# Turning attention probabilities as quarter products in an RWKV/attention/MoE block

## The chip, the cores and the metric

The kernel runs on one core of one Trainium2 chip. Its time is the device time of one launch; for the kernel before it is 640.22 us, the median of three runs (640.09 to 640.49).

## The reference

One decoder layer on 256 tokens of width 1024, in float32. `h = rms_norm(x)` goes through one input projection whose columns feed three mixers: causal pooling, RWKV-7 time mixing (8 heads of 64) and sparse attention (16 query heads, 4 key/value heads; compressed blocks, selected blocks and a sliding window). The mixers are projected, gated and summed, then comes a mixture of 32 experts. What the change touches is in the middle of it:

```
ls = einsum('bghqd,bgqkd->bghqk', qb, k_sel) + bias_s          # scores
ps = masked_softmax(ls, mask_s)                                # probabilities
o_s = einsum('bghqk,bgqkd->bghqd', ps, v_sel)                  # weighed values
...
def step(state, inp):                                          # RWKV-7, one token
    r_t, w_t, k_t, v_t, kk_t, a_t = inp
    sa = einsum('bhvk,bhk->bhv', state, -kk_t)
    state = state * w_t + sa * (kk_t * a_t) + v_t * k_t
    return state, einsum('bhvk,bhk->bhv', state, r_t)
```

The probabilities come out of the softmax with queries on the partitions, and the product with the values contracts over keys, so they have to be transposed ("turned") first. The RWKV recurrence is computed in tiles of 128 tokens with products of 64x64, and also needs some of its operands turned.

## The kernel before

Five instruction streams (TensorE = PE, VectorE = DVE, ScalarE = ACT, GpSimd = POOL, SyncE = SP) are written out by hand in one fixed order each, and meet at semaphores. Matmul results go to eight PSUM banks of 128x512 float32. A table, `plan`, made by the calls `hand(name, bank)`, says which result takes which bank and as which user of it; `begin(name)` lets PE wait until all earlier users of the bank are released (`bank_free`), `end` marks it full (`bank_full`), and the reader (ACT through `give`, or DVE) releases it after its last read.

Attention works in 24 units, slots n = 0 to 23 (`UNITS`, six for each of four groups of heads, u = n mod 6). A slot n on PE holds, in this order:

1. `early(step)`: the first half of an RWKV step, in most slots products of 64x64 (`chunkwise` on line 846, `products` on 968, line 810, line 826);
2. `turn(g, u)`: the four 128x128 blocks of slot n's probabilities `prob` turned into bank 2 (line 955, inside `turned`);
3. half of this slot's share of the merge gate products (`gate_matmuls`, lines 620, 128x128 tiles with 256 columns, two records each in the trace);
4. `late(step)`: the second half of the RWKV step, again 64x64 or 128x128;
5. in odd slots `weigh` (line 1004, values times turned probabilities); in even slots `scores` (line 984) of slots n+2 and n+3 into banks 0 and 1, both of which have to be free before the first;
6. the other half of the gates and `after(step)`.

In every sixth slot (u = 0) a further RWKV step stands ahead of this. ACT in slot n does its part of the RWKV step, then `exps(n+1)` (line 1609), then copies the turned probabilities of n from the bank (line 1435, `tok<-bank`) and releases it. DVE in slot n does its RWKV part, then `gated(n+1)` (the product that makes `prob` of n+1 final, line 1810 `tok<-tok,small`), then `logits(n+2)` (line 2038), which reads the scores of n+2 and releases their bank.

The RWKV tiles are i = 0 and 1. The step "turn" has an early part, two groups of four transposes (`bf`, `kf`, into banks 5 and 6), which ACT copies to `btok` and `ktok`, and a late part, two more groups into banks 7 and 5. For tile 0 it stands ahead of all slots, at 140 us; for tile 1 it is the step of slot 6.

Of the kernel before, what the change touches and what calls it, by code (L numbers as in the profile page):

```python
# [22 lines left out]
F32 = mybir.dt.float32  # L23
# [4 lines left out]
P = 128  # L28
D = 1024
S = 256  # L30
NT = S // P
# [5 lines left out]
DH = 64  # L37
# [147 lines left out]
def build_layer(nc, x, params, consts, front, experts, g_final, out, bias_rows):  # L185
    ctx = ExitStack()
    with ctx:
# [151 lines left out]
        gdiag = gspread[:, 1, :]  # L339
        gchan = small[:, 224:232]  # L340

        bank = [ctx.enter_context(nc.psum_tensor(f"bank{b}", [P, 512], F32)) for b in range(8)]
        total = [[bank[2], bank[6]], [bank[3], bank[7]]]


# [37 lines left out]
        def hand(name, b):  # L383
            assert name not in plan
            plan[name] = (b, nth(b))
# [19 lines left out]
        hand("ks", 0)  # L405
        hand("kcb", 7), hand("vcb", 6)
        hand("bonus0", 4), hand("bonus1", 5)

        def hand_early(step):
            if step is None:  # L410
# [76 lines left out]
        for n, (g, u) in enumerate(UNITS):  # L487
            if u == 0:
                step = next(steps)
                if g == 0:  # L490
                    hand("cT", 2)
                hand_early(step)
                hand_late(step)
                hand(f"o{g}", 7 if g == NG - 1 else 3)
                hand_gates(next(slot))
                hand_after(step)
            step = next(steps)
            hand_early(step)
            hand(f"pT{g}{u}", 2)
            hand_late(step)  # L500
            if n % 2 == 0 and n + 2 < len(UNITS):
                hand("s%d%d" % UNITS[n + 2], 0), hand("s%d%d" % UNITS[n + 3], 1)
            hand_gates(next(slot))
            hand_after(step)
# [8 lines left out]
        hand("places", 5)  # L513

        before_loop = [nth(b) for b in range(8)]


        def full(eng, name):
# [72 lines left out]
        def _(pe):  # L591
# [193 lines left out]
            def early(step):  # L785
                if step is None:
                    return
                kind, i, which = step
                ts = slice(i * P, (i + 1) * P)
                if kind == "turn":  # L790

                    if i == 0:
                        pe.wait_ge(q["rwkv_ready"], 1)
                    for w_, src in enumerate((bf, kf)):
                        turned(f"tok{i}{w_}", [src[:, m, ts] for m in range(4)])
                elif kind == "products":
                    products(i, 0)
                elif kind == "level":
                    n = which
                    pe.wait_ge(q["x_ready"], 5 * i + n + 1)  # L800
                    pe.wait_ge(q["lmask_ready"], 6 * i + n + 2)
                    chunkwise((f"W{i}{n}", lmask[(n + 1) % 2], xinv, 0, 1))
                elif kind == "local":
                    pe.wait_ge(q["xu_ready"], 2 * (i + 1))
                    rbank = [begin(f"rx{i}{c}") for c in range(2)]
                    for h in range(RH):
                        m, p = h // 2, h % 2
                        for c in range(2):
                            rows = slice(64 * c, 64 * c + 64)
                            last = pe.matmul(rbank[c][64 * p:64 * p + 64, m * CH:(m + 1) * CH],  # L810
                                             rhs[rows, h, 0, :], amat[rows, h, 1, :], start=True, stop=True)
                            if h == RH - 1:
                                end(last, f"rx{i}{c}")
                elif kind == "scan":
                    n = 2 * i + which
                    pe.wait_ge(q["rx_ready"], 2 * (i + 1))
                    pe.wait_ge(q["fc_ready"], n + 1)
                    pe.wait_ge(q["zeroed"], 3)
                    if n:
                        pe.wait_ge(q["state_ready"], n)  # L820
                    if n < NCH - 1:
                        o = begin(f"st{i}{which}")
                        for h in range(RH):
                            m, p = h // 2, h % 2
                            rows = slice(64 * p, 64 * p + 64)
                            last = pe.matmul(o[rows, m * DH:(m + 1) * DH], fc[rows, which, m, 0, :],
                                             state[rows, n % 2, m, :], start=True, stop=True)
                        end(last, f"st{i}{which}")
                elif kind == "finish":
                    pe.wait_ge(q["lora_g_ready"], 1)  # L830
                    o = begin(f"gup{i}")
                    for m in range(4):
                        last = pe.matmul(o[:, m * P:(m + 1) * P], pr("g_up", 96)[:, m * P:(m + 1) * P], mix[0:96, 13, ts],
                                         start=True, stop=True)
                    end(last, f"gup{i}")
# [115 lines left out]
            def turned(name, parts):  # L951

                o = begin(name)
                for b, part in enumerate(parts):
                    last = pe.transpose(o[:, b * P:(b + 1) * P], part, ident)  # L955
                end(last, name)

            def products(i, pair):

                obank = [begin(f"A{i}{pair}{p}") for p in range(2)]  # L960
                for mm_ in range(2):
                    m = 2 * pair + mm_
                    for j, left in enumerate((bf, kf)):
                        for c in range(2):
                            ts = slice(i * P + 64 * c, i * P + 64 * c + 64)
                            for p in range(2):
                                rows = slice(64 * p, 64 * p + 64)
                                last = pe.matmul(obank[p][64 * c:64 * c + 64, mm_ * 256 + j * P:mm_ * 256 + (j + 1) * P],  # L968
                                                 left[rows, m, ts], ar[rows, m, i, :, 64 * c:64 * c + 64],
                                                 start=True, stop=True)  # L970
                                if mm_ == j == c == 1:
                                    end(last, f"A{i}{pair}{p}")
# [16 lines left out]
            def turn(g, u):  # L989

                n = g * 6 + u
                pe.wait_ge(q["prob_ready"], n + 1)

                turned(f"pT{g}{u}", [prob[:, n % 2, s * P:(s + 1) * P] for s in (0, 2, 1, 3)])

            def weigh(g, u, o):

# [435 lines left out]
        def _(act):  # L1433
# [5 lines left out]

            count = {}  # L1440

            def give(ins, name, job):

                count[name] = count.get(name, 0) + 1
                ins.then_inc(q[name], 1)
                act.wait_ge(q[name], count[name])
                act.sem_inc(bank_free[plan[job][0]], 1)  # L1447

            def to_hT(n):

# [107 lines left out]
            def early(step):  # L1558
                if step is None:
                    return  # L1560
                kind, i, which = step
                if kind == "turn":
                    for w_, dst in enumerate((btok, ktok)):
                        b0 = full(act, f"tok{i}{w_}")
                        give(copy(dst, b0[:, :]), "tok_ready", f"tok{i}{w_}")
                elif kind == "level":
                    name = f"W{i}{which}"
                    b0 = full(act, name)
                    give(copy(winv, b0[:, :].rearrange("p (h t) -> p h t", h=RH)), "w_ready", name)
                elif kind == "solve":  # L1570
                    b0 = full(act, f"w0{i}")
                    give(copy(rhs[:, :, 1, :], b0[:, :].rearrange("p (h v) -> p h v", h=RH)), "rhs_ready", f"w0{i}")
# [70 lines left out]
            for n, (g, u) in enumerate(UNITS):  # L1643
                if u == 0:
                    step = next(steps)
                    gate_tanh(gates_done(next(slot) - 1))
                    if g == 0:
                        turned_compressed()
                    early(step)
                    late(step)  # L1650
                step = next(steps)
                gate_tanh(gates_done(next(slot) - 1))
                early(step)
                if n + 1 < len(UNITS):
                    exps(*UNITS[n + 1])
                b0 = full(act, f"pT{g}{u}")
                give(copy(probT[:, n % 2, :], b0[:, :]), "probT_ready", f"pT{g}{u}")
                late(step)
            gate_tanh(gates_done(DURING - BEFORE - 1))

# [142 lines left out]
        def _(dve):  # L1803
# [221 lines left out]
            def logits(g, u):  # L2025
# [2 lines left out]
                p = u % 2  # L2028
                b0 = full(dve, f"s{g}{u}")
                if n >= 2:  # L2030
                    b, cnt_ = plan[f"pT{(n - 2) // 6}{(n - 2) % 6}"]
                    dve.wait_ge(bank_full[b], cnt_ + 1)
                nb, w = (4, P) if u < 2 else (2, S)
                for b in range(nb):
                    bs = slice(b * w, (b + 1) * w)
# [483 lines left out]
```

## Time and profile before

| | |
|---|---|
| median of 3 runs | 640.22 us |
| the profiled execution | 640.59 us, span of its instructions 638.8 us |
| PE busy | 596.5 us, 93% of the span |
| DVE busy | 216.1 us, 34% |
| ACT busy | 142.7 us, 22% |
| HBM read | 157.07 MB, 248 GB/s over the span |
| mean granted TensorE clock | 0.977 of full speed |

The span is divided into 40 slices on the profile's page; attention lies in slices 12 to 21; the experts' weights come in from slice 22 on, at up to 425 GB/s. Times of instructions are microseconds from the span's start. A matmul in float32 has two records in the trace, a transpose has one; matmuls overlap, so what a group costs is read from its start to the start of what follows, not from the sum of its durations. The tile in the array (as 64*64) stands ahead of the shape.

### The profile page before, as it was taken

The page shows a single profiled execution, that of the slowest core. Times are in us where ns is not written, and L with a number is a line of the kernel's source. Part 1 is how long each engine was busy: PE and PEld are TensorE (multiplying, and loading weights), DVE is VectorE, ACT ScalarE, POOL GpSimd, SP SyncE. Part 2 cuts the span into 40 slices and gives each one's busy share as a digit, 9 for nine tenths or more (in the row PEclk, how much of TensorE's full clock was granted, in tenths as well). Part 3 has the DMA queues.
Part 4 walks back from the last instruction along what each step waited for, and adds up shares of the span by engine and source line. Part 5 has one row for each costly group of instructions (what it writes and reads, how often), then busy time and mean ns, then how long its engine had stood idle before and what let it go on. Part 6 is the DMA issues. An engine that isn't in the chain of part 4 may idle for free.

```text
span 638.8 us, 11809 instructions
## 1 busy us (share of the span) xinstructions
PE 596.5 (93%) x4968; PEld 432.8 (68%) x4968; DVE 216.1 (34%) x586; ACT 142.7 (22%) x366; POOL 19.9 (3%) x23
## 2 busy tenths in 40 slices
PE   8999999999999999999999999998988988958694
PEld 7988887878877877778888888884434533414331
DVE  3152448625334766356220322233111111101022
ACT  3110234042234453444330000001110111000023
POOL 1000000000200103001000000000000000000000
PEclk9999999999999999999999999998999989969798
DMA  8584344841211121102336997978999999999993
GB/s 326 196 324 171 124 145 158 316 139 67 88 47 69 68 68 68 68 27 107 122 97 261 422 421 280 425 315 313 424 419 419 422 420 421 420 421 421 422 390 123
DMA packets 27416, 158.95 MB, mean 249 GB/s; under 512 B 3025, under 2 KB 7265, under 8 KB 9569
## 3 DMA queue, kind: packets, MB, share of 16 engines
q1 hardware_dynamic: 24352, 137.71, 55.1%
q10 hardware_dynamic: 3008, 20.45, 7.7%
q8 instruction: 41, 0.67, 0.4%
q14 instruction: 15, 0.11, 0.1%
HBM read 157.07 MB, written 1.07 MB: 248 GB/s over the span
## 4 chain that ended last, share of the span: by engine, by line
PE 61%; issue 22%; DMA 7%; SPq 4%; DVE 3%; ACT 2%; POOL 0%; POOLq 0%; DVEq 0%; ACTq 0%
PE bank L620 27%; PE bank L1235 7%; DMA ring<-experts 6%; PE bank L1299 4%; SPq L583 4%; PE bank L1244 4%; PE bank L1308 3%; PE bank L846 3%; PE bank L652 2%; PE bank L955 2%; PE bank L984 2%; PE bank L1004 1%; DVE work L1810 1%; PE bank L968 1%; DMA table<-params 1%
## 5 line engine op out<-in xcount | busy, mean ns | idle before, releaser
L620 PE MATMUL bank<-hT,ring 128*128 128x256 f32 x864 | 199.4, 383 | 0.4 <-ACTq L1447 0.3
L620 PEld LDWEIGHTS bank<-hT,ring 128*128 128x128 f32 x864 | 159.6, 190 | 30.4 <-issue 10.6
L620 PE MATMUL bank<-yT,ring 128*128 128x256 f32 x256 | 55.4, 379 | 0.0
L620 PEld LDWEIGHTS bank<-yT,ring 128*128 128x128 f32 x256 | 48.6, 190 | 6.6
L1810 DVE TENSOR_TENSOR work<-bank,table 128x512 f32<-128x512 f32 (+1 forms) x22 | 11.6, 544 | 97.2 <-PE bank L1244 90.5
L1299 PE MATMUL bank<-ring,work 128*32 128x512 f32 (+1 forms) x192 | 36.0, 667 | 7.8 <-DMA yT<-experts 6.6
L1244 PEld LDWEIGHTS bank<-work,tok 128*128 128x128 f32 x256 | 31.0, 196 | 10.2 <-issue 10.2
L1435 ACT ACTIVATE work<-bank 128x512 f32<-128x512 f32 (+2 forms) x45 | 23.4, 519 | 55.1 <-PE bank L1299 42.5
L1244 PE MATMUL bank<-work,tok 128*128 128x128 f32 x256 | 32.5, 282 | 0.5 <-DVEq L2319 0.5
L1308 PE MATMUL bank<-work 128*128 128x512 f32 (+1 forms) x68 | 30.4, 584 | 1.3 <-ACT work L1435 0.7
L1609 ACT ACTIVATE tok<-tok,small 128x128 f32<-128x128 f32 (+1 forms) x64 | 28.5, 445 | 12.5 <-DVE small L2038 10.5
L1235 PE MATMUL bank<-ring,work 128*32 128x512 f32 x240 | 29.7, 607 | 0.0
L620 PE MATMUL bank<-ring,work 128*128 128x256 f32 (+1 forms) x144 | 29.0, 358 | 0.0
L620 PEld LDWEIGHTS bank<-ring,work 128*128 128x128 f32 x144 | 24.9, 190 | 2.8
L1308 PEld LDWEIGHTS bank<-work 128*128 128x128 f32 x68 | 12.0, 189 | 19.8 <-issue 17.0
L1817 DVE SCALAR_TENSOR_TENSOR work<-work,bank 128x256 f32<-128x256 f32 x8 | 3.4, 421 | 64.3 <-ACT work L1752 64.3
L1435 ACT ACTIVATE hT<-bank,table 128x128 f32<-128x128 f32 x12 | 3.6, 367 | 91.8 <-PE bank L1139 86.1
L1817 DVE SCALAR_TENSOR_TENSOR work<-ring,bank 128x512 f32<-128x512 f32 x12 | 8.3, 688 | 43.1 <-PE bank L620 43.1
L1299 PEld LDWEIGHTS bank<-ring,work 128*32 128x32 f32 x192 | 8.9, 124 | 19.2 <-issue 16.5
L1624 ACT ACTIVATE ring<-bank,small 128x256 f32<-128x256 f32 x24 | 10.1, 470 | 52.7 <-PE bank L620 52.6
L2038 DVE CUSTOM_DVE_ANT_0 tok<-bank,ring 128x128 f32<-128x128 f32 (+1 forms) x64 | 19.6, 352 | 6.4 <-PE bank L984 6.2
L1299 PE MATMUL bank<-hT,work 128*32 128x512 f32 x24 | 15.4, 805 | 6.5 <-DMA ring<-experts 6.5
(258 smaller groups left out, 720.3 us busy)
## 6 DMA issues: line engine op xcount, KB each, us to landing
ring<-front SPq DMA_DIRECT2D x47, 1024.0 KB, 5.0
ring<-experts SPq DMA_DIRECT2D x40, 1024.0 KB, 24.3
work<-experts SPq DMA_DIRECT2D x9, 1024.0 KB, 27.6
ring<-experts ACTq DMA_DIRECT2D x8, 1024.0 KB, 14.8
table<-experts SPq DMA_DIRECT2D x6, 1024.0 KB, 26.9
yT<-experts SPq DMA_DIRECT2D x6, 1024.0 KB, 26.8
hT<-experts SPq DMA_DIRECT2D x4, 1024.0 KB, 24.6
work<-experts ACTq DMA_DIRECT2D x3, 1024.0 KB, 27.8
```

The lines of the kernel that those rows point to most:

```text
L583: sp.dma_start(part, whole).then_inc(q[f"late_loaded{p}"] if p else loaded[slot_of(c)], 16)
L620: return first(pe.matmul(o, l, r, start=(k == 0), stop=(k == n - 1)))
L652: return first(pe.matmul(o[0:cols, col + i * P:col + (i + 1) * P], w[:, k, lo:lo + cols], hT[:, k, i * P:(i + 1) * P], start=(k == lo == i ...
L846: last = pe.matmul(o[to, h * CH:(h + 1) * CH], left[rows, h, :], right[rows, h, :], start=True, stop=True)
L1235: last = pe.matmul(bank[4][CAP * e:CAP * (e + 1), :], gath[:, k, CAP * e:CAP * (e + 1)], w[:, e, :], start=(k == 0), stop=(k == KD - 1))
L1244: last = pe.matmul(o, tok[:, i, k * P:(k + 1) * P], sel[:, i, :], start=(i == 0), stop=(i == 1))
L1299: last = pe.matmul(o[CAP * e:CAP * (e + 1), 0:w], ghidT[:, f, CAP * e:CAP * (e + 1)], down[e][:, f, lo:lo + w], start=(f == 0), stop=(f == 1))
L1308: return pe.matmul(total[i][lo // 512][:, lo % 512:lo % 512 + w], wselT[:, i, :], ydown[:, lo:lo + w], start=False, stop=(gang == NGANG - ...
L1435: return act.activation(o, i_, ACT.Copy, scale=scale)
L1609: ins = act.activation(pb, pb, ACT.Exp, scale=-1.0, bias=astat[:, 8 * (n % 2) + b:8 * (n % 2) + b + 1], accum_out=astat[:, 16 + 8 * (n % 2 ...
L1810: return dve.tensor_tensor(o, a, b, op)
L2038: ins = dve.tensor_tensor_reduce(prob[:, n % 2, bs], b0[:, bs], back, 1.0, FAR, ALU.add, ALU.min, astat[:, 8 * (n % 2) + b:8 * (n % 2) + b ...
```

## The change

In slots whose early part consists of 64x64 products (n = 0, 1, 2, 4, 5, 8, 10, 11, 12, 13, 15, 16) and in slot 6, which turns the second RWKV tile, the four transposes of 128x128 are replaced by `quartered`: each 128x128 block is multiplied, in quarters, with a 64x64 identity, 16 products of 64x64 for the four blocks. Products that read partitions 0 to 63 write one bank, those that read 64 to 127 a second one. The second bank (`pU`) is bank 1 for even u and bank 0 for odd u, banks that otherwise hold scores. PSUM is declared as one tensor with the banks placed so that bank 2 lies between banks 0 and 1, and ACT copies both halves with one instruction over two banks; it waits for both and releases both. DVE's logits of n+2 wait for both. The early part of the RWKV step "turn" is quartered as well, for both tiles: 32 products instead of 8 transposes, the first bank with the lower rows of both operands and the second with the upper ones, and both full only at the end.

```diff
+        banks = ctx.enter_context(nc.psum_tensor("bank", [P, 8 * 512], F32))
+        seat_of = (0, 2, 1, 3, 4, 5, 6, 7)
+        bank = [banks[:, n * 512:(n + 1) * 512] for n in seat_of]
...
+        def upper_bank(step, u):
+
+            if step is None or step[0] in ("seed", "solve", "finish") or step == ("scan", NT - 1, 1):
+                return None
+            return 0 if u % 2 else 1
...
             hand(f"pT{g}{u}", 2)
+            if upper_bank(step, u) is not None:
+                hand(f"pU{g}{u}", upper_bank(step, u))
...
-                    for w_, src in enumerate((bf, kf)):
-                        turned(f"tok{i}{w_}", [src[:, m, ts] for m in range(4)])
+                    quartered((f"tok{i}0", f"tok{i}1"), [src[:, m, ts] for src in (bf, kf) for m in range(4)])
...
+            def quartered(names, parts):
+
+
+                into = [begin(name) for name in names]
+                for b, part in enumerate(parts):
+                    for c in range(2):
+                        for r in range(2):
+                            rows = slice(64 * r, 64 * r + 64)
+                            to = slice(64 * (c ^ r), 64 * (c ^ r) + 64)
+                            last = pe.matmul(into[r][to, b * DH:(b + 1) * DH], part[rows, to], ident[rows, rows],
+                                             start=True, stop=True)
+                            if c == 1 and b == len(parts) - 1:
+                                end(last, names[r])
...
-                turned(f"pT{g}{u}", [prob[:, n % 2, s * P:(s + 1) * P] for s in (0, 2, 1, 3)])
+                parts = [prob[:, n % 2, s * P:(s + 1) * P] for s in (0, 2, 1, 3)]
+                if f"pU{g}{u}" in plan:
+                    quartered(neighbours(f"pT{g}{u}", f"pU{g}{u}"), parts)
+                else:
+                    turned(f"pT{g}{u}", parts)
...
-                b0 = full(act, f"pT{g}{u}")
-                give(copy(probT[:, n % 2, :], b0[:, :]), "probT_ready", f"pT{g}{u}")
+                if f"pU{g}{u}" in plan:
+                    names = neighbours(f"pT{g}{u}", f"pU{g}{u}")
+                    give(copy(probT[:, n % 2, :].rearrange("p (b r t) -> p r b t", r=2, t=DH), halves_of(names, 0, 256)),
+                         "probT_ready", *names)
+                else:
+                    b0 = full(act, f"pT{g}{u}")
+                    give(copy(probT[:, n % 2, :], b0[:, :]), "probT_ready", f"pT{g}{u}")
```

How the instructions stand on PE ahead of the slots, before. `bank<-table,work` are the turns of the first RWKV tile (the identity lies in `table`, the operands in `work`); in square brackets are the semaphores waited for.

```order
L955 MATMUL bank<-table,work 128x128 [waits bank_free5,rwkv_ready]
L955 MATMUL bank<-table,work 128x128 x3
L955 MATMUL bank<-table,work 128x128 [waits bank_free6]
L955 MATMUL bank<-table,work 128x128 x3
L955 MATMUL bank<-table,work 128x128 [waits bank_free7]
L955 MATMUL bank<-table,work 128x128 x3
L955 MATMUL bank<-table,work 128x128 [waits bank_free5]
```

The same place now; line 955 of before is line 975, and line 987 is the new function.

```order
L987 MATMUL bank<-table,work 64x64 [waits bank_free6,bank_free5,rwkv_ready]
L987 MATMUL bank<-table,work 64x64 x31
L975 MATMUL bank<-table,work 128x128 [waits bank_free7]
L975 MATMUL bank<-table,work 128x128 x3
L975 MATMUL bank<-table,work 128x128 [waits bank_free5]
```

The first two groups have become one of 32 products, which wants banks 5 and 6 at once; the fourth still wants bank 5 back.

Slot 0 and slot 1 on PE, before: `bank<-table,tok` turns the probabilities, which lie in `tok`.

```order
L846 MATMUL bank<-t,vraw 64x64 [waits bank_free5,lmask_ready,x_ready]
L846 MATMUL bank<-t,vraw 64x64 x15
L955 MATMUL bank<-table,tok 128x128 [waits bank_free2,prob_ready]
L955 MATMUL bank<-table,tok 128x128 x3
L620 MATMUL bank<-hT,ring 128x256 [waits slot_loaded3] x2
...
L984 MATMUL bank<-ring 128x256 [waits bank_free1,bank_free0]
L984 MATMUL bank<-ring 128x256 x3
```

Now (lines 866, 987, 641 and 1018 for 846, 955, 620 and 984):

```order
L866 MATMUL bank<-t,vraw 64x64 [waits bank_free5,lmask_ready,x_ready]
L866 MATMUL bank<-t,vraw 64x64 x15
L987 MATMUL bank<-table,tok 64x64 [waits bank_free1,bank_free2,prob_ready]
L987 MATMUL bank<-table,tok 64x64 x15
L641 MATMUL bank<-hT,ring 128x256 [waits slot_loaded3] x2
...
L1018 MATMUL bank<-ring 128x256 [waits bank_free1,bank_free0]
L1018 MATMUL bank<-ring 128x256 x3
...
L987 MATMUL bank<-table,tok 64x64 [waits bank_free2,bank_free0,prob_ready]
```

The turn waits for a second bank, 1 in slot 0 and 0 in slot 1, and the score products behind it, whose own list is the same, now come after a user of bank 1 that ACT has to release.

## Rows read from the trace of the kernel before

**Rows 1.** busy us of PE, PEld, DVE, ACT, POOL; granted clock; DMA share; GB/s

```profile
184.00:210.00 26.00, 26.00 (x509) 20.38 (x505) 11.99 (x45) 12.81 (x36) 0.00 (x0) 1.00 0.13 44
520.00:600.00 80.00, 61.86 (x440) 27.97 (x436) 9.37 (x24) 7.38 (x18) 0.00 (x0) 0.89 1.01 421
```

**Rows 2.** waits of PE, 170 to 430 us: total us, times, longest

```profile
PE bank L1004 <- ACT tok L1435: 0.4, 1, 0.4
...
PE bank L955 <- DVE tok L1810: 0.2, 1, 0.2
```

**Rows 3.** timeline of PE, slots 0 and 1: start us, us, engine, line, operation

```profile
176.97 1.15 PE L846 MATMUL bank<-t,vraw 64*64 64x64 f32 x32
178.05 0.66 PE L955 MATMUL bank<-table,tok 128*128 128x128 f32 x4
178.54 1.03 PE L620 MATMUL bank<-hT,ring 128*128 128x256 f32 x4
179.50 0.27 PE L846 MATMUL bank<-t,vraw 64*64 64x64 f32 x2
...
180.59 1.13 PE L984 MATMUL bank<-ring 64*128 64x256 f32 x8
181.66 1.56 PE L620 MATMUL bank<-hT,ring 128*128 128x256 f32 x6
183.15 1.15 PE L846 MATMUL bank<-t,work 64*64 64x64 f32 x32
```

**Rows 4.** timeline of PE, slot 5 and the first of group 1

```profile
207.54 1.16 PE L941 MATMUL bank<-work,ring 64*64 64x64 f32 x64
208.52 0.65 PE L826 MATMUL bank<-table,t 64*64 64x64 f32 x16
...
213.67 0.68 PE L826 MATMUL bank<-table,t 64*64 64x64 f32 x16
214.28 1.13 PE L620 MATMUL bank<-hT,ring 128*128 128x256 f32 x4
215.34 0.68 PE L914 MATMUL bank<-table,work 64*64 64x64 f32 x16
```

**Rows 5.** timeline, copy of slot 0's turned probabilities on ACT

```profile
180.43 0.57 ACT L1435 ACTIVATE tok<-bank 128x512 f32<-128x512 f32 x1
```

**Rows 6.** timeline of all engines, first RWKV tile's turn

```profile
138.52 1.53 DVE L1810 TENSOR_TENSOR work<-bank,work 128x512 f32<-128x512 f32 x2
...
140.26 2.02 PE L955 MATMUL bank<-table,work 128*128 128x128 f32 x16 [0.23 <-DVEq L1988]
140.92 1.31 ACT L1435 ACTIVATE t<-bank 128x512 f32<-128x512 f32 x2 [0.23 <-PE bank L955]
...
142.11 0.60 PE L955 MATMUL bank<-table,xcmp 128*128 128x128 f32 x4
```

**Rows 7.** timeline of all engines, slot 6 with the second tile's turn

```profile
216.92 1.46 PE L620 MATMUL bank<-hT,ring 128*128 128x256 f32 x6
...
218.22 1.04 PE L955 MATMUL bank<-table,work 128*128 128x128 f32 x8
...
218.85 1.31 ACT L1435 ACTIVATE t<-bank 128x512 f32<-128x512 f32 x2 [7.87 <-PE bank L955]
...
221.79 1.13 PE L984 MATMUL bank<-ring 64*128 64x256 f32 x8
221.84 0.57 ACT L1435 ACTIVATE tok<-bank 128x512 f32<-128x512 f32 x1
```

**Rows 8.** timeline of all engines, slot 10

```profile
242.53 0.66 PE L955 MATMUL bank<-table,tok 128*128 128x128 f32 x4 [0.18 <-DVE tok L1810]
...
242.74 0.41 DVE L2038 CUSTOM_DVE_ANT_0 tok<-bank,ring 128x256 f32<-128x256 f32 x1
```

**Rows 9.** timeline of all engines, slot 12

```profile
263.72 0.57 ACT L1435 ACTIVATE tok<-bank 128x512 f32<-128x512 f32 x1
...
263.87 1.13 PE L984 MATMUL bank<-ring 64*128 64x256 f32 x8
```
## What the change does to the time: the prediction

> **What bounds the kernel now.** I read the stages first. In the attention stage (about 176 to 340 us, the stretch that the change touches, with one earlier place at 140 us) PE is busy for all of 26.00 us in the stretch shown, DVE for 12.0 and ACT for 12.8, and the granted clock is 1.00, so TensorE runs at 2.4 GHz throughout; in the expert stage the DMA engines are busy all the time (share 1.01) and PE is not [rows 1]. Then the waits of PE: between 170 and 430 us only a few short ones stand, the longest 0.4 us for a copy by ACT and 0.2 us for a product by DVE [rows 2]. So attention is a stream of PE instructions without a hole: a microsecond added to the stream, or a wait put into it, comes out at the stage's end. The expert loads (ACT's and SP's DMAs) begin only as attention and then the branch products give their buffers back, and from then on the DMA is the limit, so all of that stage moves by the same amount as the attention's end. I pass a delay on one to one. The opposite case, that the DMA stage swallows it, would need loads that start before attention is over, and the loads into attention's buffers can't.
>
> Then the timeline of single slots, which carries the prices. I call the 24 slots by n = 0 to 23.
>
> **Part 1: the stream itself.** The turn was four transposes of 128x128; it becomes 16 products of 64x64. Price of a quarter product: line 941's 32 products of 64x64, which go round all four quadrants as the new ones do, take 207.54 to 208.52 us until the next line in the same tile size, 0.98 us or 30.6 ns each [rows 4]. So 16 cost 0.49 us. The four transposes took 178.05 to 178.54, 0.49 us too [rows 3]. Nothing is gained there.
>
> What is left is the switch of tile size, which the change does not remove but moves behind the turn. Line 846's 16 products on two quadrants last 1.08 us until the first transpose [rows 3]; line 826's 8 until a gate product last 0.61 [rows 4]. The difference gives 0.059 us each, so 0.94 of the 1.08 is work and 0.14 the switch. The gate products behind it show a second part: two of them (four records) take 178.54 to 179.50, 0.96 us, behind transposes [rows 3], but 214.28 to 215.34, 1.06 us, right behind 64x64 products [rows 4]. Before: 1.08 + 0.49 + 0.96 = 2.53. After: 0.94 + (0.49 + 0.14) + 1.06 = 2.63. That is +0.10 us a slot; over the twelve slots that turn no RWKV tile (n = 0, 1, 2, 4, 5, 8, 10, 11, 12, 13, 15, 16) +1.2 us. Bounds: nothing, if quarter products overlap the tail of line 846's on the idle quadrants, to +0.15.
>
> The Trainium skill ("TensorEngine Tiling (Array Packing)", Key Properties) says that changing the tiling mode drains the engine. By that rule alone, with as many changes as before in these twelve slots, this term would be zero and the sum below 4.2 us. The rows show that what stands behind a switch matters as well, and I take the rows.
>
> **Part 2: the first RWKV tile's turn.** Eight transposes into banks 5 and 6 become 32 quarter products, 0.98 us. The last one ends some 0.24 us after it starts (records of such products last 0.22 to 0.27 [rows 3]), so ACT's copies, which began at 140.92, start at about 141.48; one takes 0.66 at most by the pair's 1.31 [rows 6], 0.60 for the first without the second's overlap. Bank 5 is then free near 142.25: the release comes after the copy, and DVE's release of this same bank took from 140.05 (138.52 + 1.53) to PE's start at 140.26, 0.21 us [rows 6]; for ACT I take 0.15 (bounds 0.05 and 0.21). Line 955's fourth group, which needs bank 5, waits for that and takes 0.46, a quarter of the 1.85 us that sixteen transposes took from 140.26 to 142.11: 142.71 against 142.11 [rows 6], +0.60.
>
> **Part 3: slot 6, the second tile's turn.** Six gate records take 1.30 us from 216.92 to the transposes [rows 7], and 1.49 from 181.66 to 64x64 products [rows 3]; 0.10 of the difference is the price above of following a smaller tile, so a switch into 64x64 costs 0.09. Quarter products begin at 218.31, the last starts 0.95 later and ends near 219.48, so ACT copies from 219.50 instead of 218.85: +0.65. ACT is then busy without a gap (two copies, four exponentials) up to the copy of slot 6's probabilities, which was at 221.84 for 0.57 [rows 7]; it ends now at 223.06. This copy also has to free bank 1, the score bank that holds the upper rows, and line 984 (scores of slots 8 and 9) wants banks 0 and 1. It began at 221.79 [rows 7], its stream comes by 222.2, but the bank is free at 223.2. Slot 6: +1.43.
>
> **Part 4: scores wait for the copy.** Behind the waiting score products stand the rest of the gates and the next slot, all of PE. In slot 0 the copy ends at 180.43 + 0.57 = 181.00 [rows 5], free 181.15; the scores started at 180.59 [rows 3] and would come at 180.69: a wait of 0.46. Slot 12: 263.72 + 0.57, free 264.44, against 263.87 + 0.10 [rows 9]: 0.47. In slots 2, 4, 8, 10 and 16 the copy is out of the way by then. Sum 0.93.
>
> **Part 5: the turn waits for DVE.** The upper half goes into a bank whose scores DVE reads one step later than the probabilities just turned: DVE computes the product for slot n and only then the logits of slot n+1, and the turn of n now wants the latter's bank. In slot 10 DVE is late: PE already waited 0.18 us and started the turn at 242.53, while the last logits run 242.74 + 0.41 = 243.15 [rows 8]; with the release 243.36, a wait of 0.83. Four more slots show the same picture, worked out in the same way: n = 2 (0.17), 11 (0.27), 13 (0.03 once slot 12's wait has moved PE but not DVE) and 16 (0.34). In the other eight the bank is long free. Sum 1.64. In slot 11 the 0.4 us that PE waited for ACT [rows 2] shrinks by the 0.37 put in before it: -0.37.
>
> ACT's copy of two banks with 64-element runs has as many elements as before and is not dearer by any row; DVE's wait for both banks is no news to it. Both are priced at nothing, hidden behind PE.
>
> **Sum.** 1.2 + 0.60 + 1.43 + 0.93 + 1.64 - 0.37 = 5.4 us. The profiled execution took 640.59 (span 638.8 and 1.8 around it), the median of the runs is 640.22; the difference is carried over: **645.6 us**. Its own range is 643.3 to 647.4: the stream's term between nothing and +1.8, releases at 0.05 to 0.21 at some seven places.
>
> **Rivals.**
> *Waits absorbed, only the stream is longer.* PE delays in one slot give DVE and ACT time to catch up, so that the waits of parts 4 and 5 mostly vanish, and slot 6 costs its stream alone (+0.41), the first tile +0.27. For it: slot 13 behaves so. Against: the late operand in slots 0, 6, 10 and 12 is made inside the slot, after PE's own small products, and moves with PE. 1.2 + 0.7 = 1.9: 642.1.
> *The switch is saved (faster).* The place is the end of the early products: if the 0.14 us there is the price of entering transposes, not of leaving 64x64, the quarter products drop it, and gates behind them cost 0.96. That is 0.14 in each of twelve slots, 1.7 us, provided the banks' waits don't come; the point is whether the gates follow quarter products at once. It would be 638.5. Against it: line 826 into a gate product pays the same (0.61, then 1.06) with no transpose near [rows 4].
> *Waits compound.* DVE stands at its limit around slot 10, where its work since the products of slot 8 has no gap; if scores that come late make its logits late, and those the exponentials and the copy that now frees the next score pair, each of five slots costs 0.8 us more: 649.6. For it: the new loop scores, logits, exponentials, copy, scores closes over two slots. Against: a slot is some 6 us (176.97 to 183.15 [rows 3]), two are 12, and of the loop's work the scores take 1.07 (180.59 to 181.66 [rows 3]), the copy 0.57 [rows 5], the two logits some 0.8 [rows 8] and the exponentials no more than the 1.7 us between the two other copies and the last one in slot 6 [rows 7].
> *The banks are never in the way*, the change doing only what it says with equal cost: 640.2.
>
> **Chances.** Forecast 0.66, absorbed 0.16, compounding 0.08, no difference 0.05, faster 0.05. A measurement of this kernel tells about 0.2% (1.3 us) from no change; so slower by more than that 0.90, within it 0.05, faster 0.05. The range reaches to the absorbed case and most of the way to the compounding one: 641.8 to 648.2.
>
> **What the next profile would show.** The 64x64 turns 0.49 us long for 16, gates behind them 1.06 instead of 0.96; new waits of PE: score products for ACT's copy in slots 0, 6 and 12, the turn for DVE's logits in slot 10 foremost; the end of attention 5 us later and the expert stage as long as it was. I am wrong if PE shows no such waits, or if the quarter products run well below 30 ns each.

## The result, and the profile after

The changed kernel takes 646.11 us (median of 4, 645.5 to 647.64) against 640.36 (median of 4, 640.09 to 640.97): a ratio of 1.0091, interval 1.0078 to 1.0104. It is 5.75 us slower; 5.4 were forecast, and 645.6 us. In the session of e9 to e11 one run of e11 (886 us) and two of the kernel before (887 and 3434 us) stand far outside the others and are left out of the medians.

The profiled execution of it took 647.64, 7.0 more by the span than that of before. Of these, 1.3 lie ahead of everything the change touches: the first RWKV tile's turn starts at 141.57 instead of 140.26. The waits of PE before that point name `DMA ring<-front`, 0.4 and 0.2 us, which stand in no wait of before, and the other kernels below start the same turn anywhere from 140.49 to 141.35 us. So I measure the attention from the start of that turn to the start of the last turned probabilities (slot 23). In the timeline of PE that last turn is, before and after (start us, us, engine, line, operation, tile, shape, count):

```profile
335.76 0.60 PE L955 MATMUL bank<-table,tok 128*128 128x128 f32 x4
```

```profile
342.75 0.60 PE L975 MATMUL bank<-table,tok 128*128 128x128 f32 x4
```

Before: 335.76 - 140.26 = 195.50. After: 342.75 - 141.57 = 201.18, +5.68. From there to the end of the span it is 303.04 us before (638.8 - 335.76) and 303.05 after: the delay passes to the end one to one. That the two agree to 0.01 is chance: in the other kernels below this last stretch takes 301.6 to 302.6 us. One to one is shown to some 1.5 us by the traces; the medians, 5.75 against 5.68, say the same. "By the trace" below is the change of this stretch against 195.50.

The page of the changed kernel, its span and its instruction fetches (packets, MB, share); before there were 11809 instructions and 41 packets:

```profile
span 645.8 us, 12788 instructions
...
q8 instruction: 45, 0.74, 0.5%
```

The two largest waits of PE in the attention (total, times, longest). Neither existed before, apart from 0.18 us in slot 10, where the turn then waited for DVE's product; they answer to [rows 2]:

```profile
PE bank L1018 <- ACTq L1486: 2.1, 3, 1.0
PE bank L987 <- DVEq L2093: 1.2, 2, 1.0
```

Slot 0 on PE, against [rows 3]. The early products take 0.94 until the quarter products begin (179.75), these 0.61 until the gates (forecast 0.63), together 1.55 where it had been 1.57, and the scores (183.11) stand still 0.53 us for ACT:

```profile
178.81 0.97 PE L866 MATMUL bank<-t,vraw 64*64 64x64 f32 x26
...
179.75 0.68 PE L987 MATMUL bank<-table,tok 64*64 64x64 f32 x27
180.36 1.13 PE L641 MATMUL bank<-hT,ring 128*128 128x256 f32 x4
...
183.11 1.14 PE L1018 MATMUL bank<-ring 64*128 64x256 f32 x8 [0.53 <-ACTq L1486]
...
185.67 0.97 PE L866 MATMUL bank<-t,work 64*64 64x64 f32 x26
```

ACT's copy of both banks in that slot, against [rows 5]. It ends at 182.85, and the scores start 0.26 later:

```profile
182.28 0.57 ACT L1473 ACTIVATE tok<-bank 128x512 f32<-128x512 f32 x1
```

Slot 5, a slot without any wait, against [rows 4]: 3.16 us from line 961 to line 934, where it had been 3.01 (207.54 to 210.55).

```profile
210.49 1.16 PE L961 MATMUL bank<-work,ring 64*64 64x64 f32 x64
...
212.59 1.13 PE L641 MATMUL bank<-hT,ring 128*128 128x256 f32 x4
213.65 0.68 PE L934 MATMUL bank<-table,work 64*64 64x64 f32 x16
```

The first tile's turn, against [rows 6]. 32 quarter products take 0.98 (142.66 is 1.09 with the switch), ACT starts its copies 1.20 after their start instead of 0.66, and the fourth group waits for bank 5, inside the second row. To line 641 it is 2.82 us, before it was 2.29:

```profile
141.57 1.16 PE L987 MATMUL bank<-table,work 64*64 64x64 f32 x64 [0.18 <-issue]
...
142.66 1.46 PE L975 MATMUL bank<-table,work 128*128 128x128 f32 x8
142.77 1.31 ACT L1473 ACTIVATE t<-bank 128x512 f32<-128x512 f32 x2 [0.72 <-PE bank L987]
...
144.39 0.81 PE L641 MATMUL bank<-hT,ring 128*128 128x256 f32 x3
```

Slot 6, against [rows 7]. ACT's first copy starts 1.21 behind the first quarter product (before 0.63), its last copy ends at 226.18, the scores start at 226.44 after standing for 1.03:

```profile
221.41 1.16 PE L987 MATMUL bank<-table,work 64*64 64x64 f32 x64
...
222.39 0.65 PE L987 MATMUL bank<-table,tok 64*64 64x64 f32 x32
...
222.62 1.31 ACT L1473 ACTIVATE t<-bank 128x512 f32<-128x512 f32 x2 [8.69 <-PE bank L987]
...
225.61 0.57 ACT L1473 ACTIVATE tok<-bank 128x512 f32<-128x512 f32 x1
...
226.44 1.14 PE L1018 MATMUL bank<-ring 64*128 64x256 f32 x8 [1.03 <-ACTq L1486]
```

Slot 10, against [rows 8]. DVE's last logits end at 247.77, PE's turn starts 0.22 after that and had stood for 1.00:

```profile
247.36 0.41 DVE L2090 CUSTOM_DVE_ANT_0 tok<-bank,ring 128x256 f32<-128x256 f32 x1
...
247.99 0.69 PE L987 MATMUL bank<-table,tok 64*64 64x64 f32 x32 [1.00 <-DVEq L2093]
```

### The profile page after: what moved, and what is told of

The parts are those of the page before. It is cut to its first block, busy times and chain, and to the rows that moved or that the text cites. A ratio compares the mean times of both kernels' runs of the same rounds, so it can differ in the third digit from the quotient of the medians.

```text
span 645.8 us, 12788 instructions
## 1 busy us (share of the span) xinstructions
PE 598.0 (93%) x5444; PEld 433.6 (67%) x5444; DVE 216.4 (34%) x586; ACT 142.7 (22%) x366; POOL 19.8 (3%) x23
## 4 chain that ended last, share of the span: by engine, by line
PE 56%; issue 22%; DMA 10%; SPq 4%; DVE 3%; ACT 3%; POOL 0%; POOLq 0%; DVEq 0%; ACTq 0%
PE bank L641 24%; PE bank L1273 7%; DMA work<-experts 4%; PE bank L1282 4%; PE bank L1346 4%; DMA ring<-front 4%; PE bank L1337 3%; PE bank L866 3%; SPq L604 3%; DMA ring<-experts 2%; PE bank L673 2%; PE bank L1018 2%; PE bank L987 1%; ACT tok L1655 1%; PE bank L1042 1%
## 5 line engine op out<-in xcount | busy, mean ns | idle before, releaser
L1473 ACT ACTIVATE t<-bank 128x512 f32<-128x512 f32 x16 | 9.6, 597 | 48.8 <-PE bank L866 29.2
```

Source lines behind the costliest of these rows:

```text
L1473: return act.activation(o, i_, ACT.Copy, scale=scale)
```

## The experiments

Theory: the change costs because the second bank is one that others need, so PE waits for releases (3.3 us of the 5.7), and because two tile turns and the changes of tile size lengthen the stream. Rivals: the quarter products are dear in themselves, or the waits only show where PE would stand anyway. The medians scatter by about 1 us, and the kernel before had 640.09 us in the session of e1 to e4, 640.91 in that of e5 to e8 and 640.19 in that of e9 to e11, so medians are compared by their ratios and each run is also read by the trace.

| run | median us | ratio to before (95%) | by the trace |
|---|---|---|---|
| changed kernel | 646.11 | 1.0091 (1.0078 to 1.0104) | +5.68 |
| e1_bank0 | 644.55 | 1.0067 (1.0051 to 1.0082) | +3.90 |
| e2_tiles_back | 645.70 | 1.0087 (1.0070 to 1.0104) | +5.12 |
| e3_tiles_only | 641.61 | 1.0026 (1.0015 to 1.0037) | +1.28 |
| e4_copy_first | 644.88 | 1.0075 (1.0057 to 1.0093) | +4.58 |
| e5_three_cuts | 644.05 | 1.0047 (1.0031 to 1.0063) | +3.60 |
| e6_joined | 644.70 | 1.0054 (1.0040 to 1.0068) | +2.93 |
| e7_joined_transposes | 642.85 | 1.0032 (1.0020 to 1.0045) | +2.89 |
| e8_two_cuts | 644.03 | 1.0047 (1.0035 to 1.0060) | +3.70 |
| e9_slot16_back | 643.25 | 1.0047 (1.0031 to 1.0062) | +2.55 |
| e10_release_order | 645.89 (one run) | none | +5.53 |
| e11_two_bank_transposes | 643.30 | 1.0048 (1.0029 to 1.0067) | +3.42 |

### Another bank: e1_bank0

```diff
-            return 0 if u % 2 else 1
+            return 0
```

> The changed kernel (646.1 us), with one thing other: the second bank of the turned probabilities is bank 0 in every slot, also where u is even. In even slots bank 0 is free long before the turn, since the logits of the slot itself have released it; bank 1 is free only after the logits of the slot behind. My theory (the turn waits for DVE's release of bank 1): the waits of the turn in slots 2, 10 and 16 go, 0.2, 0.8 (0.18 of the 1.0 was there before the change) and 0.3 us, together 1.3 us, so 644.8; the score products of slots 0, 6 and 12 wait as before for ACT's copy, which now frees bank 0. Rival (the cost lies in the stream of quarter products and tile sizes, waits only show it elsewhere): 646.1, with the idle time turning up in front of the next product of the same slot.

In slot 10 PE is back at the wait it had before the change:

```profile
246.05 0.69 PE L987 MATMUL bank<-table,tok 64*64 64x64 f32 x32 [0.18 <-DVE tok L1861]
```

The waits of the turn for DVE's release are gone, and the attention is 1.78 us shorter than in the changed kernel. 1.3 was expected; the rest comes from the scores, which now wait 0.37, 0.88 and 0.37. In slot 0 the copy ends at 182.33 and the scores start only 0.10 later, not 0.26:

```profile
181.76 0.57 ACT L1473 ACTIVATE tok<-bank 128x512 f32<-128x512 f32 x1
...
182.43 1.13 PE L1018 MATMUL bank<-ring 64*128 64x256 f32 x8 [0.37 <-ACTq L1486]
```

The theory holds: the waits of part 5 in even slots were caused by the choice of bank 1, and nearly nothing came in their place; 0.1 us came back, in slot 13.

### The tiles' turns as before: e2_tiles_back

```diff
-                    quartered((f"tok{i}0", f"tok{i}1"), [src[:, m, ts] for src in (bf, kf) for m in range(4)])
+                    for w_, src in enumerate((bf, kf)):
+                        turned(f"tok{i}{w_}", [src[:, m, ts] for m in range(4)])
...
```

> The changed kernel with the early turn of both RWKV tiles as it was, eight transposes of 128x128 into banks 5 and 6, and the probabilities quartered as in the changed kernel. My theory: the first tile gives back 0.53 us. In slot 6 the copies of ACT start 0.65 us earlier, so the copy that frees the score bank does too: of the 1.55 us that the slot grew by, 0.8 remain (the copy ends at 222.41 in the time of the kernel before, and the scores started at 221.79). Sum -1.3, so 644.8. Rival (the tile turns cost no more than they did, ACT is late in slot 6 by itself): no change from 646.1 beyond 0.3.

```profile
PE bank L1019 <- ACTq L1487: 1.5, 3, 0.5
...
PE bank L988 <- DVEq L2093: 1.2, 2, 1.0
```

By the trace the slots up to 15 run 1.0 us ahead of the changed kernel (the turn of slot 15 at +4.03 instead of +5.01), the scores of slot 6 wait 0.42 instead of 1.03; expected were 1.3. Then 0.4 of it is given back in slot 16, where PE stands behind the quarter products without a releaser, and 0.56 remain. The median moved by 0.4, which its interval doesn't tell from nothing. That stop in slot 16 is taken up with e8 and e9.

### The tiles' turns alone: e3_tiles_only

```diff
         def upper_bank(step, u):
-            if step is None or step[0] in ("seed", "solve", "finish") or step == ("scan", NT - 1, 1):
-                return None
-            return 0 if u % 2 else 1
+            return None
```

> Only the RWKV tiles' early turns quartered, all probabilities turned by transposes into bank 2 as before the change. My theory: +0.53 for the first tile (PE waits for bank 5), and in slot 6 only the longer stream, 0.09 for the switch into 64x64, 0.98 instead of 0.87 for the products and 0.17 for the way back, +0.4; no wait, since the scores' banks are not in use. Sum +0.9: 641.3. Rival (the tile turns are what delays ACT, and through it the whole of the attention): +2 or more, 642.4.

+1.28 by the trace and 1.5 by the medians; the first tile and slot 6 behave as expected, and 0.3 come on top in slot 7. There ACT is still late from slot 6, and the gate products, whose bank it has to release (its last read of it ends at 227.14), start 0.75 us behind the transposes instead of 0.44:

```profile
226.58 0.60 PE L973 MATMUL bank<-table,tok 128*128 128x128 f32 x4
227.33 1.10 PE L639 MATMUL bank<-hT,ring 128*128 128x256 f32 x4
```

So a late ACT is paid for once, by the scores where these wait for it anyway, or else by the gates a slot later. By the trace the rival's 2 us is out; the interval of the medians, up to 1.0037, alone would still allow it.

### The copy first: e4_copy_first

```diff
-                if n + 1 < len(UNITS):
-                    exps(*UNITS[n + 1])
                 if f"pU{g}{u}" in plan:
                     ...
+                if n + 1 < len(UNITS):
+                    exps(*UNITS[n + 1])
```

> The changed kernel, with ACT copying the turned probabilities of a slot ahead of the exponentials of the next slot instead of behind them, in all 24 slots. My theory (score products wait in slots 0, 6 and 12 because the copy that frees the score bank stands behind four exponentials of 0.39 us): these waits, 0.53, 1.03 and 0.53 us, go, and nothing comes in their place, since the exponentials are needed a slot later: 646.1 - 2.1 = 644.0. Rival (ACT's order doesn't matter, its delay comes back with the exponentials, DVE's product and so with the turn of the next slot): 646.1, the turn waiting for prob_ready in slots 1, 7 and 13.

The three waits of the scores are gone, 2.1 us, as the theory said. Only 1.1 of it arrive. In slot 7 the gates wait for ACT's release of their bank, as in e3:

```profile
226.88 0.84 ACT L1670 ACTIVATE ring<-bank,small 128x256 f32<-128x256 f32 x2
...
227.91 1.10 PE L641 MATMUL bank<-hT,ring 128*128 128x256 f32 x4 [0.19 <-ACTq L1486]
```

and in slot 13 the turn, no longer held back by slot 12's scores, stands until DVE's logits are read (270.25 + 0.42, and the release):

```profile
270.25 0.42 DVE L2090 CUSTOM_DVE_ANT_0 tok<-bank,ring 128x256 f32<-128x256 f32 x1
...
270.84 0.69 PE L987 MATMUL bank<-table,tok 64*64 64x64 f32 x32 [0.34 <-issue]
```

Slot 1 gives back 0.1 in the same way as slot 13. In slot 23 the attention loses another 0.25, and there the turn does wait for DVE's product of the late exponentials, the rival's own path; the turn stands at 340.57, where its weights wait 0.49 for it:

```profile
340.56 0.42 PEld L975 LDWEIGHTS bank<-table,tok 128*128 128x128 f32 x4 [0.49 <-DVE tok L1861]
```

The rival is right in half: half of the time comes back, in slots 1, 7 and 13 through releases of banks and only in slot 23 through `prob_ready`. My forecast had counted on that in the other direction when it set slot 13's wait to 0.03.

### The waits alone: e11_two_bank_transposes

Transposes of 128x128 as before, but two of the four into the second bank, which ACT copies and releases with the first; no quarter products anywhere.

```diff
+                    for r in range(2):
+                        for b in range(2):
+                            last = pe.transpose(into[r][:, b * P:(b + 1) * P], parts[2 * r + b], ident)
+                        end(last, names[r])
...
```

> The kernel before with its transposes of 128x128, but in the change's thirteen slots two of the four go into the second bank, 1 or 0 as in the change, and ACT copies and releases both; the tiles' turns are transposes into banks 5 and 6 as before. So the bank waits without the quarter products. My theory, from the trace of before and 0.3 us from the end of a copy to its second release: scores wait 0.7 in slot 0, 0.9 in 6 and 0.7 in 12, the turn 0.8 in slot 10, 0.06 in 2 and 0.25 in 16, and the waits of slots 11 and 13 are swallowed by others: +3.5, so 643.9. Rival (the waits exist only since quarter products end late): +1 or less, 641.4.

```profile
PE bank L1019 <- ACTq L1492: 2.0, 3, 0.8
...
PE bank L1035 <- DVEq L2100: 1.2, 2, 1.0
...
PE bank L1048 <- ACT tok L1479: 0.3, 1, 0.3
```

+3.42 by the trace, 3.1 by the medians. These are the changed kernel's waits, place for place (0.61, 0.81 and 0.60 for ACT; 1.03 and 0.17 for DVE). So the second bank alone costs 60% of what the change costs, whatever is written into it. With e3's 1.28 for the tiles' turns, 0.98 of the 5.68 is left for the quarter products of the slots themselves, and twelve slots that grow by some 0.08 each make 1.0.

### Two and three cuts: e8_two_cuts, e5_three_cuts

e8 is e1's and e2's edits together, e5 these and e4's.

> The changed kernel with the second bank always bank 0 and the RWKV tiles turned by transposes; ACT's order as it was. My theory (the two costs stand in different slots and add up): 646.1 less 1.8 for the bank and 1.0 for the tiles as the traces of the two single cuts have them, 643.3; the score products still wait for ACT's copy in slots 0, 6 and 12, 0.35 each. Rival (a wait taken away in one slot comes back in another): 644.3 or more.

> Twelve slots and slot 6 with quartered probabilities as in the change, but with the three costs taken away that the runs so far showed: second bank always bank 0, the RWKV tiles turned by transposes, and ACT's copy of the turned probabilities ahead of the exponentials. My theory (waits for banks are most of the change's cost, the stream with its tile sizes the rest): 12 slots of 0.08 to 0.15, slot 6 0.35, slot 11 0.3 and slot 13 0.4 for DVE, less the 0.4 that PE waited for ACT in slot 11 before the change, and some tenths where ACT's later exponentials come up: +2 from 640.1, so 642.1. Rival (quarter products are dear by themselves, their weight loads stand in the way of the gates'): +3.5 or more, 643.6.

Up to slot 15 e8 is at +2.37, where the sum of the single cuts from the changed kernel's +5.01 would give +2.6: they add up. Then it loses 1.3 us in slot 16, and ends at +3.70 where the theory had 2.9; its median lies between the theory's and the rival's. PE's timeline there:

```profile
285.89 1.16 PE L962 MATMUL bank<-work,ring 64*64 64x64 f32 x64
286.87 0.59 PE L847 MATMUL bank<-table,t 64*64 64x64 f32 x14
...
287.92 0.48 PE L641 MATMUL bank<-hT,ring 128*128 128x256 f32 x1
289.20 0.92 PE L641 MATMUL bank<-hT,ring 128*128 128x256 f32 x3 [0.80 <-issue]
```

288.40 to 289.20 is no wait for a semaphore. e5 has the same stop in slots 16 and 5, 0.34 us each, another of 0.24 in slot 15, besides a wait of 0.34 in slot 13 like e4's, and ends at +3.60, so of three waits of scores, 1.0 us together, 0.1 was gained. The theory's +2 for e5 was too low. The rival's +3.5 is what the trace gives (the medians say 3.1), yet not for the rival's reason: where they don't overlap the early products, the quarter products themselves still took 0.57 to 0.67 up to the gates.

### Slot 16 by transposes: e9_slot16_back

```diff
-            if step is None or step[0] in ("seed", "solve", "finish") or step == ("scan", NT - 1, 1):
+            if step is None or step[0] in ("seed", "solve", "finish") or (step[0] == "scan" and step[1] == NT - 1):
...
```

> The kernel with bank 0 and the tiles' transposes (the one with two costs taken away, 644.0 us), with slot 16 turned by transposes too. In that kernel PE stood still for 0.8 us in slot 16, right behind the quarter products, for nothing that the trace shows but its own instructions. My theory (PE runs out of instructions: 64 short products, 16 of them quarters, go by there in under 2 us, and the next block of instructions has not landed): the gap goes, and the slot's 0.1 of stream with it, so the attention ends 0.9 earlier by the trace, about 643.1. Rival (the gap belongs to the gate product behind it, or to the place in the program): it stays, 643.9, or turns up at slot 16's scores.

The same stretch without quarter products:

```profile
285.68 1.16 PE L962 MATMUL bank<-work,ring 64*64 64x64 f32 x64
286.67 0.65 PE L847 MATMUL bank<-table,t 64*64 64x64 f32 x16
287.25 0.66 PE L976 MATMUL bank<-table,tok 128*128 128x128 f32 x4
287.74 1.03 PE L641 MATMUL bank<-hT,ring 128*128 128x256 f32 x4
288.70 0.68 PE L935 MATMUL bank<-table,work 64*64 64x64 f32 x16
```

No stop there or later, and the attention is 1.15 us shorter than e8's. (The medians, 643.25 and 644.03 in two sessions, have the same ratio to before.) In e8 the stop follows the quarter products: 56 products of 64x64 (32 of line 962, 8 of 847, 16 quarters) go by in 2.0 us ahead of it. But such a run doesn't stop PE by itself. In e1 the same 56 go by in slot 16 in the same 2.0 us, without a wait, and the gates follow at once:

```profile
286.79 1.19 PE L961 MATMUL bank<-work,ring 64*64 64x64 f32 x64
...
288.24 0.66 PE L987 MATMUL bank<-table,tok 64*64 64x64 f32 x30
288.83 1.13 PE L641 MATMUL bank<-hT,ring 128*128 128x256 f32 x4
```

e1 and e8 differ only in the tiles' turns, which give the program another length ahead of this place, so the rival's "place in the program" stays possible. So does chance, as each kernel was traced once: in gate products at 116 us, far ahead of any quarter product and in code that e6, e8 and e9 share, a stop of the same sort takes 0.28, 0.17 and 0.46 us. That the medians don't show e9's gain of 1.15 speaks for chance too. That PE is short of instructions fits, but isn't shown: in e8 the one instruction packet near the stop moved at about 286.7, before it. The changed kernel has no such stop in slot 16; DVE's wait of 0.18 there is no reason for it, since e2 has the same wait and loses 0.4 all the same.

### The order of the releases: e10_release_order

```diff
-                         "probT_ready", *names)
+                         "probT_ready", f"pU{g}{u}", f"pT{g}{u}")
```

> The changed kernel, with ACT releasing the upper bank before bank 2 behind the copy of both. In even slots the changed kernel released bank 2 first and bank 1 second. My theory (each release that ACT issues stands behind the one before, some 0.15 us): the score products' waits in slots 0, 6 and 12, 0.53, 1.03 and 0.53 us, shrink by 0.15 each, to what they were with bank 0, which was released first: 0.37, 0.88 and 0.37; the attention is 0.3 to 0.45 shorter by the trace. Rival (bank 0's shorter waits came from DVE's earlier release of it): 0.53, 1.03, 0.53 as before.

```profile
182.01 0.57 ACT L1473 ACTIVATE tok<-bank 128x512 f32<-128x512 f32 x1
...
182.78 1.13 PE L1018 MATMUL bank<-ring 64*128 64x256 f32 x8 [0.47 <-ACTq L1486]
```

The waits are 0.47, 0.97 and 0.46, each 0.06 shorter, and copy to scores takes 0.20 instead of 0.26. A release in front costs 0.06, not 0.15. The further 0.10 that bank 0 has over bank 1 (e1) remains open; both theories miss it, as DVE's release of bank 0 was long past. The order in which PE itself waits for the two banks is a rival that no run changes.

### Gates moved away: e6_joined, e7_joined_transposes

In the level slots, on top of e5 (e6) and of the kernel before (e7):

```diff
+                joined = step is not None and step[0] == "level"
+                if not joined:
                     gate_matmuls(share[:len(share) // 2])
                 late(step)
...
+                if joined:
+                    gate_matmuls(share[:len(share) // 2])
                 gate_matmuls(share[len(share) // 2:])
```

> The kernel with the three costs taken away, and in the seven slots whose step is a level of the RWKV solve (0, 1, 2, 10, 11, 12, 13) the gate products that stood between the turn and the late 64x64 products moved behind the scores or the weighing. Then early products, quartered turn and late products are one stretch of 64x64 tiles. My theory (each change of tile size costs 0.1 to 0.14 us on either side, and the quartered turn had only moved it): such a slot loses one change into 64x64 and one out of it, 0.3 us, and gets a wait of 0.2 for ACT's copy of the early result, which the gates had covered: -0.1 a slot, some -0.7 against the kernel without the move, so 641.4. Rival (tile size matters little, the gates were there as cover): +0.2 or more a slot, 643.5.

> The kernel before the change, with the same move of gate products behind the scores or the weighing in its level slots, and all turns by 128x128 transposes. The number of changes of tile size stays as it was (the transposes now stand between the 64x64 groups), the cover is gone. My theory: +0.2 us a slot for the wait for ACT's copy, and in odd slots the weighing may wait longer for the turned probabilities, 0.4 to 0.8 us, since their copy stands behind the exponentials: +3 in all, 643. Rival (the move gains by itself, whatever the turn): below 640.

e6, waits of PE:

```profile
PE bank L641 <- issue: 1.0, 2, 0.7
PE bank L867 <- ACT t L1478: 0.9, 4, 0.2
PE bank L867 <- ACTq L1491: 0.7, 2, 0.4
```

By the trace e6 gains 1.03 us over e5 up to slot 16 and loses 0.36 of it to a longer stop there, which leaves 0.67, the forecast 0.7. By the medians (644.70 against 644.05, overlapping intervals) it is no gain, so this is shown in the traces only. e7 has the same move without quarter products and loses 2.89 us, forecast 3, most of it in the weighing, which waits for the turned probabilities:

```profile
PE bank L1004 <- ACT tok L1439: 2.0, 3, 1.1
```

By the traces joining pays in e6, where the turn between the 64x64 groups is 64x64 too, and not in e7; even so e6 stays above the kernel before. The two differ in more than the turn, though: e6 has e5's order of ACT, with the copy ahead of the exponentials, and the 2.0 us that e7's weighing waits are for that copy. Without them e7 would still lose 0.9, an estimate; a run of e7 with ACT's order of e6 is missing, so how much of the difference is the tile size isn't shown. No version that was run beats the kernel before, so none is put forward.

## Why the prediction was right

The measured 5.68 us by its steps, from the traces:

- Part 1, stream: forecast 0.10 a slot. Slots 1, 4, 8, 13 and 15, which hold no wait, grew by 0.08 to 0.10, slot 5 by 0.15. The rule of the Trainium skill that the prediction names ("TensorEngine Tiling (Array Packing)", Key Properties), that changing the tiling mode drains the engine, gave zero for these slots when only the changes are counted, and falls short. That the gates follow a smaller tile is what the rows gave, and slot 5 shows it: its four gate records take 1.06 us (212.59 to 213.65), as long as behind 64x64 products in [rows 4], where behind transposes in [rows 3] they had taken 0.96.
- Part 2, first tile: 0.60 forecast, 0.53 measured.
- Part 3, slot 6: 1.43 forecast, 1.55 measured; the mechanism is the one described, with 1.03 us of standing. Slot 7, which the prediction left out, gets 0.10 shorter.
- Part 4, scores: 0.46 and 0.47 forecast, 0.60 each measured (the idle time in front of the instruction is 0.53). The release was priced at 0.15 from the end of the copy and takes 0.26 when it is the second one; bounds of 0.05 to 0.21 were too narrow. The same 0.11 makes up nearly all of slot 6's 0.12.
- Part 5, turn for DVE: slot 10 grew by 1.06 with its stream (forecast 0.93), slot 2 by 0.29 (0.27), slot 16 by 0.49 (0.44), slots 11 and 13 by 0 and 0.08. e1 removes those of the even slots.
- One to one to the end: 303.04 and 303.05 us, equal within the 1.5 us by which this stretch differs between kernels.

The mechanism is the one forecast, place for place; part of the closeness of the sum is luck. Scores, slot 6 and the turns for DVE cost some 0.6 us more than forecast, the stream, the first tile and slot 7 some 0.3 less, which leaves 0.3. And the stop without a releaser, which I did not foresee at all, costs 0.8 us in e8's trace and happens not to occur in the changed kernel's. The rival of absorbed waits is answered by e4, e1 and e11: half of the waits that e4 removes comes back elsewhere and next to nothing of e1's, and a wait that is added is paid in full where nothing else stands behind it. The rival of the saved switch would have needed gates at 0.96 behind quarter products.

## What to carry to other kernels

A change that borrows a buffer has to be priced by who releases it and how late, before what it does inside is priced: here the bank cost 3.4 us, the tiles' turns 1.3 and the quarter products themselves 1.0. Splitting a product into smaller tiles next to other small tiles saves no change of tile size unless the large ones between the groups go too. When a wait is taken out of a full stream, look up what comes second in the same place; in e4 about half of it was there, in e1 almost nothing.

## What the runs showed of the hardware

- 64x64 products on four quadrants follow each other in 30.6 ns (32 in 0.98 us), on two in 59 (16 in 0.94 us, slot 0 of the changed kernel); a turn of four 128x128 blocks costs 0.49 us either way, before the gates behind it pay 0.10 more for following the smaller tile.
- PE can stand still without a releaser behind a dense run of short products: 0.8 us behind 56 of them in 2.0 us (e8), but nothing behind the same 56 in e1, and nothing behind 40 and four transposes (e9). The cause is not shown; the place in the program and chance in the one trace of each kernel both stay possible.
- From the end of ACT's copy of two banks to the start of a waiting product: 0.26 us when the bank was released second, 0.20 when first, and 0.10 when it was bank 0. DVE's release took 0.22 in slot 10 and 0.17 in slot 13 of e4.
